# Second part's u and z in seven block products for eight, and the first two tiles of the last projection row by row of the weights

## What is computed

```
def sgu_mixer(h, chunk_len, w_in, ln_g, ln_b, w_s, s_bias, w_out):
    B, T, _ = h.shape
    p = h @ w_in
    uv = jax.nn.gelu(p[..., :2 * E_B], approximate=False)
    z = p[..., 2 * E_B:]
    u, v = jnp.split(uv, 2, axis=-1)
    v = layernorm(v, ln_g, ln_b)
...
    mixed = jnp.einsum('gij,bcjgd->bcigd', ws, v5)
...
    s = (u5 * mixed).reshape(B, T, E_B) * jax.nn.silu(z)
    return s @ w_out, v
```

## Time and profile before

| | us |
|---|---|
| runs | 2412.58, 2417.39, 2418.74; median 2417.39 |
| profiled execution | 2414.95 |
| its span | 2413.1 |
| TensorE, matmuls busy | 2351.5 (97%) |
| VectorE busy | 1449.3 (60%) |
| ScalarE busy | 674.6 (28%) |
| second part's `u_stage`, first start to last start of its matmuls | 1602.40 to 2022.89 |
| last projection | 2027.99 to the end |

### The profile page before, as it was taken

The page is one execution under the profiler, slowest core; times in us unless marked ns, Lnnn a source line. Parts: engine busy times, 40 slices in busy tenths (PEclk is TensorE's granted clock), DMA queues, the critical chain, the costliest instruction groups (busy, mean ns, idle before and its releaser), DMA issues.

```text
span 2413.1 us, 27653 instructions
## 1 busy us (share of the span) xinstructions
PE 2351.5 (97%) x11824; PEld 2053.7 (85%) x11824; DVE 1449.3 (60%) x1395; ACT 674.6 (28%) x955; POOL 233.4 (10%) x419
## 2 busy tenths in 40 slices
PE   7899999999999998999989999999999998999998
PEld 6788899999887887888778877889999998888885
DVE  5599999995769879999946742224334444222221
ACT  5322223222542112222324531112222333111110
POOL 1100000001211110000001210011000000000000
PEclk9999999999999999999989999999999999999999
DMA  4323244232552213333334442113222344322220
GB/s 167 122 93 100 98 136 143 94 125 76 185 192 104 95 68 106 112 101 113 126 120 140 137 147 95 65 53 100 85 86 89 116 135 166 110 97 91 92 92 22
DMA packets 113818, 265.05 MB, mean 110 GB/s; under 512 B 15776, under 2 KB 51872, under 8 KB 111648
## 3 DMA queue, kind: packets, MB, share of 16 engines
q1 hardware_dynamic: 90208, 184.64, 23.3%
q0 software_dynamic: 23488, 78.64, 9.5%
HBM read 184.86 MB, written 78.75 MB: 109 GB/s over the span
## 4 chain that ended last, share of the span: by engine, by line
PE 92%; DVE 4%; DMA 2%; ACT 1%; issue 1%; POOL 0%; SPq 0%; DVEq 0%; ACTq 0%
PE PS L1366 29%; PE PS L1367 29%; PE PS L1368 29%; PE PS L1573 3%; DVE acc L1053 2%; PE PS L1412 1%; PE PS L1434 1%; PE PS L1377 1%; DMA raw<-wa_in_in 0%; PE PS L1421 0%; DMA zb<-silu_z_scratch 0%; DMA xt<-x_in 0%; DVE m L1272 0%; DMA rawb<-wb_out_in 0%; DVE Ul L1017 0%
## 5 line engine op out<-in xcount | busy, mean ns | idle before, releaser
L1053 DVE SCALAR_TENSOR_TENSOR acc<-cp,cw,acc 128x1024 f32<-128x1024 f32 (+1 forms) x480 | 639.4, 1332 | 12.6
L1366 PE MATMUL PS<-HBh,Uh 128*128 128x512 f32 (+2 forms) x1280 | 457.6, 357 | 1.6 <-ACT vb L931 1.6
L1367 PE MATMUL PS<-HBl,Uh 128*128 128x512 f32 (+2 forms) x1280 | 453.4, 354 | 0.0
L1368 PE MATMUL PS<-HBh,Ul 128*128 128x512 f32 (+2 forms) x1280 | 453.4, 354 | 0.0
L1366 PE MATMUL PS<-HAh,Wh 128*128 128x512 f32 (+2 forms) x960 | 341.7, 356 | 0.5 <-DVE HAl L1017 0.5
L1367 PE MATMUL PS<-HAl,Wh 128*128 128x512 f32 (+2 forms) x960 | 340.0, 354 | 0.0
L1368 PE MATMUL PS<-HAh,Wl 128*128 128x512 f32 (+2 forms) x960 | 339.8, 354 | 0.0
L1366 PEld LDWEIGHTS PS<-HBh,Uh 128*128 128x128 f32 x1280 | 241.9, 189 | 23.4 <-issue 2.6
L1368 PEld LDWEIGHTS PS<-HBh,Ul 128*128 128x128 f32 x1280 | 241.6, 189 | 20.7
L1367 PEld LDWEIGHTS PS<-HBl,Uh 128*128 128x128 f32 x1280 | 241.8, 189 | 20.0 <-issue 0.2
L1366 PE MATMUL PS<-Wbh,s7h 128*128 128x512 f32 (+1 forms) x544 | 212.6, 391 | 7.4 <-DVE s7l L1017 7.4
(11 more groups left out here) (116 smaller groups left out, 3036.6 us busy)
## 6 DMA issues: line engine op xcount, KB each, us to landing
rawu<-wb_uz_in SPq DMA_DIRECT2D x64, 512.0 KB, 3.5
raw<-wa_in_in SPq DMA_DIRECT2D x48, 512.0 KB, 3.5
rawv<-wb_v_in SPq DMA_DIRECT2D x64, 256.0 KB, 4.8
v_scratch<-vb POOLq DMA_DIRECT2D x64, 256.0 KB, 2.6
vt<-v_scratch SPq DMA_DIRECT2D x32, 512.0 KB, 4.0
s_scratch<-m POOLq DMA_DIRECT2D x32, 512.0 KB, 3.9
st<-s_scratch SPq DMA_DIRECT2D x16, 1024.0 KB, 4.9
xt<-x_in SPq DMA_DIRECT2D x16, 512.0 KB, 4.4
```

The costliest lines, as they stand in the source:

```text
L1053: ins = nc.vector.scalar_tensor_tensor(out=a, in0=c[:, k:k + w], scalar=cw[:, j, k:k + 1], in1=a, op0=ALU.mult, op1=ALU.add)
L1366: nc.tensor.matmul(out, wh, xh, start=start, stop=False)
L1367: nc.tensor.matmul(out, wh, xl, start=False, stop=False)
L1368: return nc.tensor.matmul(out, wl, xh, start=False, stop=stop)
```

## The change

**Block products.** In the second part the tokens are cut in two halves of 544 (A1., A2.), the depth in two halves of 512 (.1, .2), and the weights into u and z (B.1 for u, B.2 for z) and the same two depths. C11 and C21 are u of the two halves of tokens, C12 and C22 z. Where before eight block products made them, seven do now:

| | sum of tokens | sum of weights |
|---|---|---|
| S1, T1 | A21+A22 | B22-T2 |
| S2, T2 | S1-A11 | T3+B11 |
| S3, T3 | A11-A21 | B22-B12 |
| S4, T4 | A12-S2 | B21-T2 |

Products M1=A11 B11, M2=A12 B21, M3=S4 B22, M4=A22 T4, M5=S1 T1, M6=S2 T2, M7=S3 T3. The T are sums of each block's weights, made on VectorE (`q_add_up`), the S are made once (`q_tokens`, `q_ahead`), all split in high and low. A product is done in two pieces (`sub`) of 272 tokens: 4 steps of depth times `three`, 12 matmuls. What is shared between results goes from bank to bank: ScalarE copies M1 to the bank where M6 is added on top (`copy_ab`), M1+M6 to the bank of M5 (`copy_bc`), and M7 to SBUF (`copy_m7`); M2 is added onto M1, M3 and M4 onto the sums, and VectorE adds M7 (`add_22`, `add_21`) ahead of the SiLU and GELU of those quarters.

**Last projection.** The tensors of the block products lie where rows 0 to 7 of `w_out` were loaded. All 16 rows are now loaded from the last products on, in the order `K_ORDER`, and `b_first_tiles` takes tiles 0 and 1 row by row as rows come, tile 2 from row 8 on eight rows behind.

The diff, cut to its core (`q_high` and `q_low` split a piece of weights, `q_load` loads it, `q_gate_u` and `q_gate_z` are `u_gate` in parts, `s3_...` and `s_sum_...` split the sums of tokens; the waits for semaphores that were renamed are left out):

```diff
--- before.py
+++ after.py
+TH = WIDTH[1] // 2
+GW = TH // 2
+KH = KD // 2
+SUBS = 2 * KB
+LEFT = {"M1": "A11", "M2": "A12", "M3": "S4", "M4": "A22", "M5": "S1", "M6": "S2", "M7": "S3"}
+RIGHT = {"M1": "B11", "M2": "B21", "M3": "B22", "M4": "T4", "M5": "T1", "M6": "T2", "M7": "T3"}
+SPLITS = ("T3", "B11", "T2", "T1", "B21", "B22", "T4")
+SUMS = ("T3", "T2", "T1", "T4")
+K_ORDER = (5, 0, 1, 2, 3, 4, 6, 7) + tuple(range(8, KB))
...
+        def quad_order():
+            order = [(m, 0) for m in ("M1", "M6", "M2", "M7", "M5")]
+            for sub in range(1, SUBS):
+                order += [("M1", sub), ("M7", sub), ("M3", sub - 1), ("M4", sub - 1), ("M6", sub)]
+                if sub == SUBS - 1:
+                    order += [("mix", sub // 2), ("M5", sub), ("M2", sub)]
+                else:
+                    order += [("M2", sub)] + [("mix", sub // 2)] * (sub % 2) + [("M5", sub)]
+            return order + [("M3", SUBS - 1), ("M4", SUBS - 1)]
...
+            def wb_load(i):
+                k = K_ORDER[i]
+                if k == 5:
+                    sp.wait_ge(u_mm, q_mm("M7", SUBS - 1))
                 if k == 0:
-                    sp.wait_ge(v_mm, V_DONE[1])
+                    sp.wait_ge(u_mm, q_mm("M5", SUBS - 1))
+                if k == 3:
+                    sp.wait_ge(u_mm, q_mm("M3", SUBS - 1))
+                if k == 6:
+                    sp.wait_ge(u_mm, q_mm("M4", SUBS - 1))
+                    sp.wait_ge(u_mu, q_gated(1, KB - 1))
...
+            def copy_ab(sub):
+                act.wait_ge(u_mm, q_mm("M1", sub))
+                if sub < 2:
+                    act.wait_ge(v_gel, v_last(1 + sub))
+                else:
+                    act.wait_ge(q_add, q_added("C21", sub - 2))
+                nc.scalar.activation(PS[:, 1 + sub % 2, 0:GW], PS[:, 0, 0:GW], ACT.Copy).then_inc(q_copy, 1)
...
+            def copy_bc(sub):
+                act.wait_ge(u_mm, q_mm("M6", sub))
+                if sub == 0:
+                    act.wait_ge(v_gel, v_last(3))
+                else:
+                    act.wait_ge(u_silu, q_silu("C12", sub - 1))
+                nc.scalar.activation(PS[:, 3, 0:GW], PS[:, 1 + sub % 2, 0:GW], ACT.Copy).then_inc(q_copy, 1)
...
+                for sub in range(1, SUBS):
+                    j = sub // 2
+                    silu_22(sub - 1)
+                    if sub % 2 == 0:
+                        q_high("T2", j)
+                    copy_ab(sub)
+                    copy_m7(sub)
+                    if sub % 2 == 0:
+                        q_high("T1", j)
+                        q_high("B21", j)
+                    silu_12(sub - 1)
+                    if sub % 2 == 0:
+                        q_high("B22", j)
+                        q_high("T4", j)
+                    elif j + 1 < KB:
+                        q_high("T3", j + 1)
+                        q_high("B11", j + 1)
+                    copy_bc(sub)
+                    if sub == SUBS - 1:
+                        s_high(0)
+                    gelu_11(sub)
+                    gelu_21(sub - 1)
+                b_high(0)
+                silu_22(SUBS - 1)
+                s_high(1)
+                silu_12(SUBS - 1)
+                b_high(1)
+                gelu_21(SUBS - 1)
...
+            def q_ahead(i):
+                if i == 0:
+                    q_add_up("T3", 0)
+                    q_tokens("S1a")
+                    q_tokens("S1b")
+                if i == 1:
+                    q_add_up("T2", 0)
+                    q_add_up("T1", 0)
+                    q_tokens("S1c")
+                    q_tokens("S2a")
+                if i == 2:
+                    q_add_up("T4", 0)
+                    q_tokens("S2b")
+                    q_tokens("S3a")
+                if i == 3:
+                    for b in SPLITS[0:5]:
+                        q_low(b, 0)
+                if i == 4:
+                    s_sum_low("S2")
+                    q_tokens("S3b")
+                if i == 5:
+                    q_tokens("S3c")
+                    q_tokens("S4a")
+                if i == 6:
+                    q_tokens("S4b")
+                    q_tokens("S4c")
...
+            def q_stage():
+                for part in range(2):
+                    s3_low(part)
+                s_sum_low("S1")
+                s_sum_low("S4")
+                q_low("B22", 0)
+                q_low("T4", 0)
+                for j in range(KB):
+                    if j > 0:
+                        u_mixed(1, j - 1)
+                        add_22(2 * j - 1)
+                        q_add_up("T1", j)
+                        q_add_up("T4", j)
+                        for b in ("T2", "T1", "B21"):
+                            q_low(b, j)
+                        q_gate_u(0, j - 1)
+                        add_21(2 * j - 1)
+                        q_low("B22", j)
+                        q_low("T4", j)
+                        q_gate_u(1, j - 1)
+                        q_gate_z(j - 1)
+                    add_22(2 * j)
+                    v_norm(1, j)
+                    u_add_bias(1, j)
+                    if j + 1 < KB:
+                        q_add_up("T3", j + 1)
+                    add_21(2 * j)
+                    if j + 1 < KB:
+                        q_add_up("T2", j + 1)
+                        for b in ("T3", "B11"):
+                            q_low(b, j + 1)
+                u_mixed(1, KB - 1)
+                add_22(SUBS - 1)
+                q_gate_u(0, KB - 1)
+                s_low(0)
+                b_low(0)
+                add_21(SUBS - 1)
+                q_gate_u(1, KB - 1)
+                q_gate_z(KB - 1)
+                s_low(1)
...
+            def q_product(m, sub):
+                a, b, j = LEFT[m], RIGHT[m], sub // 2
+                bank = {"M1": 0, "M2": 0, "M6": 1 + sub % 2, "M5": 3, "M3": 3, "M7": 4, "M4": 1 + sub % 2}[m]
...
+                if m in ("M6", "M2"):
+                    pe.wait_ge(q_copy, q_copied("ab", sub))
+                if m == "M5":
+                    pe.wait_ge(q_copy, q_copied("bc", sub))
+                if m == "M3":
+                    pe.wait_ge(q_add, q_added("C22", sub))
+                if m == "M4":
+                    pe.wait_ge(q_copy, q_copied("bc", sub))
+                cols = slice(GW * (sub % 2), GW * (sub % 2 + 1))
+                for k in range(KH):
+                    last = three(PS[:, bank, 0:GW], QWh[b][:, k, :], QWl[b][:, k, :], QAh[a][:, k, cols], QAl[a][:, k, cols],
+                                 k == 0 and m in ("M1", "M7"), k == KH - 1, seeded=True)
...
+            def b_first_tiles():
+                steps = []
+                for i in range(KB):
+                    steps += [(0, i), (1, i)] + [(2, i - 8)] * (i >= 8)
+                steps += [(2, i) for i in range(8, KB)]
...
+                    for c in range(2):
+                        last = b_row(t, i, c)
+                    if i == KB - 1:
+                        last.then_inc(o_main, 1)
```

More of the change, by code:

```diff
@@ L243, in build, with at @@
-        t7 = r("t7", [P, D])
-        gpb = r("gpb", [P, D])
+        def at(offset, name, shape, dt=fp32):
+            return Region(offset, top)(name, shape, dt)
+        quad_w = {"B11": w_at, "T3": w_at + 4096, "T2": w_at + 8192, "B21": w_at + 12288, "T1": w_at + 16384,
+                  "B22": r1_at + 46080, "T4": r1_at + 58880}
+        QWh = {b: at(o, f"{b}h", [P, KH, P], f32r) for b, o in quad_w.items()}
+        QWl = {b: at(o + 2048, f"{b}l", [P, KH, P], f32r) for b, o in quad_w.items()}
@@ L407, in tiled, with b_tile, x_loads @@
             return full, dram[NTILES - 1, :, j, 0:N_SAMPLE]
+        def b_tile(t):
+            return NTILES + t
+        def x_loads(slot):
+            return sum(1 for t in range(NTILES) if x_slot(t) == slot)
         def b_pair(t):
@@ new lines, in u_stage @@
+                    if j == 12:
+                        o_load_y(8)
+                        o_load_z(8)
+                        o_load_y(9)
+                        o_load_y(10)
+            def q_stage():
+                vt_load(1, 0)
+                for j in range(KB):
+                    if j + 1 < KB:
+                        for b in ("B12", "B22", "B11", "B21"):
+                            q_load(b, j + 1)
+                        vt_load(1, j + 1)
+                    if j == 14:
+                        s_load(0)
+                s_load(1)
+                for i in range(4):
+                    wb_load(i)
+                s_load(2)
+                for i in range(4, 8):
+                    wb_load(i)
@@ new lines, in q_stage @@
+            def q_stage():
+                s3_high(0)
+                copy_ab(0)
+                s3_high(1)
+                s_sum_high("S1")
+                copy_bc(0)
+                copy_m7(0)
+                gelu_11(0)
+                s_sum_high("S4")
+                q_high("B22", 0)
+                q_high("T4", 0)
+                for sub in range(1, SUBS):
```

(30 more changed lines are left out.)

622 lines of the change are left out of this document (429 added, 193 removed).

## The result

| | before | after |
|---|---|---|
| median of the runs, us | 2415.31 (2412.58 to 2418.74, 4 runs) | 2373.74 (2372.41 to 2375.49, 4 runs) |
| profiled execution, us | 2414.95 | 2372.43 |
| its span, us | 2413.1 | 2370.6 |

The account below looks back on a forecast made before the run. The prediction took TensorE's matmul pace to bound the kernel. Stream -42.8, seams +3.2 and +1.1 sum to -38.5 us: 2376.5 for a profiled execution, 2379 for a median, range 2368 to 2396, or 2364 to 2404 reaching into rivals.

Parts of the forecast that it names:

- The pace of 272 columns: TensorE's matmuls in the changed u_stage: 126.7 ns each, 113.3 for columns plus 13.4, within bounds 113.3 and 166.7.
- Columns count in sixteens: Matmul pace: widths round up to multiples of 16, so 360 and 364 both cost as 368, 166.7 ns.
- The straight lines: Alternative pace for 272 columns, drawn through 512 and 364 or 512 and 360 columns: 129 and 132 ns.
- Product by product: TensorE's stream in u_stage: 2304 matmuls (383.4 us) removed, 2688 (340.6 us) added, difference -42.8 us.
- The cover on the other engines: In each u_stage block, VectorE 17.6 and ScalarE 14.9 us fit under TensorE's 23.7; extra work costed at nothing.
- The seam from v to u: Head of u_stage: waits of 1.3, 0.5 and 2.3 us, together 4.1 where before 0.9; +3.2 us.
- The seam to the last projection: From u_stage's end: idle 1.9 and 6.9 us plus about 1.8 at the lower clock, 10.6 against 9.5; +1.1 us.
- The sum: Whole kernel: -42.8 + 3.2 + 1.1 = -38.5 us, giving 2379 us for a median.
- the likeliest case: Whole kernel: the main forecast around 2379 us, own range 2368 to 2396, chance 0.74.
- Rival 1: u_stage matmuls: a floor of 166.7 ns each makes the kernel slower, 2484 to 2486 us; chance 0.09.
- Rival 2: u_stage's chain of short steps binds, costing 1 to 2 us a block, 2395 to 2411 us; chance 0.13.
- Rival 3: u_stage matmuls: pace below 122 ns, down to 113.3, since 13.4 isn't fixed; 2343 to 2366 us; chance 0.04.

Follow-up runs that it names:

- second experiment: Kernel before with the second part's u_stage in four chunks of 272 columns in place of 364, 364, 360, without the seven-product scheme; 2420.88 us, ratio 1.0017.
- experiment 5: Kernel before with the second part's u_stage in chunks of 272, 272, 272, 136 and 136 columns; 2493.03 us, one run.
- experiment 9: Changed kernel with two extra VectorE multiplications of 384 columns ahead of the even unit's add_22 in each of blocks 1 to 15; 2380.52 us, ratio 0.9852.
- experiment 6: Changed kernel with ScalarE's high part of S4 ahead of copy_m7(0) and gelu_11(0); 2373.82 us, ratio 0.9824.
- Experiment 7: Changed kernel with tile 1's split ahead of the last SiLU on ScalarE and, with weight row 1, ahead of VectorE's last gates; 2370.27 us, ratio 0.9807.

## Why the prediction was right, point by point

- **"The pace of 272 columns", 126.7 ns.** The mechanism was right, the size 1.3 ns over: 125.4 within products, 3.5 us less over 2688 matmuls. That turns the forecast -42.8 into -46.3, and -45.6 was measured; what makes up the last 0.7 isn't known. The sum left out the 0.1 us of the first matmul behind a mixing, though the earlier trace rows show it (270 ns). Both kernels pay it 16 times, 1.6 us in each: it is why the stream before took 420.66 us and not the 419.2 of the sum, and in the difference it drops out. "Columns count in sixteens" holds at 352, 360, 364 and 368 within 1.3 ns, at either offset; 384 is 1.3 ns dearer and 272 is 1.3 cheaper within a product. The straight lines gave 129 and 132, farther off. Why 13.4 ns or about as much comes on top of the columns no run shows.
- **"Product by product".** A sixth more matmuls of a quarter fewer columns, -45.6. The second experiment shows that the scheme alone makes this, since the width costs 2.5 us by itself. That the 272 is divisible by 16 is part of why the width costs so little, by the table of experiment 5: before, 3 x 368 columns were paid for 1088, now 4 x 272.
- **"The cover on the other engines", costed at nothing.** Right: no wait of TensorE recurs from block 1 on, and the block's 23.42 us against 23.7 is the pace. The slack of the two tightest links was 0.68 and 0.72 for 0.9 and 0.8, the hand-over still in it; without it the first is 0.53. The ninth experiment shows how little that is: `add_22` 0.84 us later cost 0.39 us in every block.
- **"The seam from v to u", +3.2.** +2.6, and each wait on the engine forecast: 1.16, 0.31 and 2.05 for 1.3, 0.5 and 2.3. Moving S4 (experiment 6) took the last wait away and nothing took its place.
- **"The seam to the last projection", +1.1.** +0.8: 1.78 and 6.59 for 1.9 and 6.9, and the lower clock again behind it. Experiment 7 takes 7.0 of the 10.67, so the order of the queues, as laid out, was the cause of two thirds.
- **The sum**, -38.5, came out as -42.5 between the spans and -41.6 between the medians: the stream accounts for 2.8 of the 4.0, the seams for 0.9 and the start for 0.3. The forecast of 2379 for a median was 5.3 over. Most of the other 1.3 is from run to run: it took the median as 2.4 above the profiled execution, and for the kernel after it was 1.3. 2373.7 lies in the likeliest case's own range of 2368 to 2396.
- **Rival 1, a floor at 166.7**, is refuted: 125.4 by the kernel after, 110.6 by experiment 5. What spoke for it, that 360 is no quicker than 364, is the step of 16. The Trainium skill, page "Perfetto Trace Analysis", section "Identifying the Most-Contended Engine", judges TensorE's headroom by the busy share of weight loads, and by the share of peak FLOP/s, which the prediction did not weigh. Read as the prediction read it, the share of loads would have left no gain here. This case's traces disagree with that reading: the share is 99% or more at 166.7 and at 110.6 ns alike.
- **Rival 2, the chain binds**, did not come, by 0.5 us a block (experiment 9). **Rival 3, a pace under 122**, did not come: on top of 113.3 ns for the columns 12.1 remain.
